# Two parts of a 48-row block in one stationary of 112 columns, and expert weights in longer runs

## The reference

```python
combine = ...                      # (1024, 16): top-1 of 4 groups, then the top-2 of its 4 experts, weights normalized
y = 0
for e in range(16):
    h = silu(t @ w_gate[e]) * (t @ w_up[e])       # 1024 x 1024 @ 1024 x 256, twice
    y = y + combine[:, e:e + 1] * (h @ w_down[e])  # 256 x 1024
x = layer_norm(ALPHA * x + y, g, b)
```

## Time and profile before

| | |
|---|---|
| runs | 981.41 us median of 3 (980.06 to 983.18) |
| profiled execution | 976.16 us, its span 974.4 us |
| PE busy | 940.6 us (97% of the span) |
| DVE busy | 590.8 us (61%) |
| ACT busy | 350.9 us (36%) |
| POOL busy | 193.4 us (20%) |
| chain that ended last | PE 42% of the span, DVE 3%, DMA 1% |
| mean granted clock | 0.990 |

### The profile page before, as it was taken

How to read it: one execution, slowest core, us unless ns; L and a number is a source line. 1 busy time by engine, 2 the same in 40 slices (tenths; PEclk the granted TensorE clock), 3 DMA queues, 4 the chain that set the end, 5 groups by cost and what they waited for, 6 DMA issues and landing times. The chain is left out here.

```text
span 974.4 us, 15658 instructions
## 1 busy us (share of the span) xinstructions
PE 940.6 (97%) x5655; PEld 797.9 (82%) x5655; DVE 590.8 (61%) x1263; ACT 350.9 (36%) x737; POOL 193.4 (20%) x256
## 2 busy tenths in 40 slices
PE   7999999999999999999999999999899999999994
PEld 6899888777768888888867888879789898989883
DVE  6744341588676776756665445568353567777675
ACT  6123031345574555400025333230322334444441
POOL 0013100112241120013210000005200233342344
PEclk9999999999998999999999999999999999999998
DMA  8122010001699501700223000045888988899972
GB/s 308 63 87 87 1 66 1 1 1 51 259 412 368 174 23 34 277 15 1 87 86 134 1 1 1 1 173 218 272 278 261 316 276 296 294 323 328 316 254 81
DMA packets 67278, 151.60 MB, mean 156 GB/s; under 512 B 8720, under 2 KB 16144, under 8 KB 67216
## 3 DMA queue, kind: packets, MB, share of 16 engines
q1 hardware_dynamic: 59920, 133.82, 39.4%
q0 software_dynamic: 7296, 16.95, 4.5%
HBM read 107.62 MB, written 52.03 MB: 164 GB/s over the span
## 5 line engine op out<-in xcount | busy, mean ns | idle before, releaser
L2001 PEld LDWEIGHTS h_ps<-xgT,e_gate_up 128*128 128x128 f32 x1024 | 155.6, 192 | 4.9 <-issue 2.6
L2001 PE MATMUL h_ps<-xgT,e_gate_up 128*128 128x176 f32 x1024 | 157.1, 315 | 2.5 <-DVEq L2109 2.5
L265 PE MATMUL unit_ps<-whi,xhi 128*128 128x512 f32 (+1 forms) x256 | 97.8, 382 | 6.1 <-DVE wlo L303 6.1
L267 PE MATMUL unit_ps<-whi,xlo 128*128 128x512 f32 (+1 forms) x256 | 97.5, 381 | 0.0
L266 PE MATMUL unit_ps<-wlo,xhi 128*128 128x512 f32 (+1 forms) x256 | 97.5, 381 | 0.0
L265 PEld LDWEIGHTS unit_ps<-whi,xhi 128*128 128x128 f32 x256 | 48.4, 189 | 14.1 <-DVE xlo L347 6.0
L2144 DVE SCALAR_TENSOR_TENSOR z<-y_ps,slot_weight,x_rows 128x512 f32<-128x512 f32 (+1 forms) x64 | 45.7, 746 | 22.2 <-PE y_ps L2015 22.1
L267 PEld LDWEIGHTS unit_ps<-whi,xlo 128*128 128x128 f32 x256 | 48.3, 189 | 7.7
L266 PEld LDWEIGHTS unit_ps<-wlo,xhi 128*128 128x128 f32 x256 | 48.4, 189 | 7.5
L2013 PE MATMUL y_ps<-e_dn_hi,h_hi 128*128 128x512 f32 (+1 forms) x128 | 51.9, 405 | 0.0
L2015 PE MATMUL y_ps<-e_dn_hi,h_lo 128*128 128x512 f32 (+1 forms) x128 | 50.2, 392 | 0.0
(11 more groups left out here) (346 smaller groups left out, 2133.3 us busy)
## 6 DMA issues: line engine op xcount, KB each, us to landing
e_gate_up<-w_gu SPq DMA_DIRECT2D x16, 2048.0 KB, 10.3
e_down_raw<-w_dn SPq DMA_DIRECT2D x16, 1024.0 KB, 6.2
slot_rows<-zeros SPq DMA_DIRECT2D x22, 522.0 KB, 6.2
slot_sums<-zeros SPq DMA_DIRECT2D x22, 512.0 KB, 6.3
x_rows<-slot_rows SPq DMA_DIRECT2D x16, 522.0 KB, 4.8
slot_sums<-z SPq DMA_DIRECT2D x16, 512.0 KB, 4.4
wraw<-w_in SPq DMA_DIRECT2D x24, 256.0 KB, 4.8
xraw<-xT SPq DMA_DIRECT2D x16, 256.0 KB, 5.0
```

Of the source, the lines that this page charges most:

```text
L265: pe.matmul(o, hi, whi[:, s, 0:w], start=(s == 0), stop=False)
L267: last = pe.matmul(o, lo, whi[:, s, 0:w], start=False, stop=(s == KD - 1))
L2001: end = pe.matmul(hps[:, m, gu * CAP:(gu + 1) * CAP], gate_up[:, b, s, w], xT[:, s, :], start=(s == 0), stop=(s == KD - 1))
```

## The change

In the down product, the two units of block 1 are computed otherwise. `h_hi` is now 240 columns wide for each f: 128 of block 0, 48 of block 1, 16 of zeros, and then 48 with the *low* part of block 1. One stationary of 112 columns (128 to 240) gives high x high in PSUM rows 0 to 47 and low x high in rows 64 to 111, in one matmul; high x low follows as a second one. So a unit of block 1 has 4 matmuls in place of 6. DVE makes z of such a unit in two steps, the second of which waits for the first, and makes `h_lo` in two pieces. The order of the units is kept, with block 1's low part under a semaphore of its own.

The expert weights are laid out in DRAM so that each partition reads runs of 4096 bytes; `paired` is the matching view of the same tiles in SBUF. SP waits for `placed_at` ahead of its stores, and fetches block c of the rows of n + 2 before it stores block c of z, no longer after both stores. Left out of the diff below: the names of two semaphores, the count of `stats_cleared` that ACT waits for (7 for 6), the slice `hhi[:, m, 0:CAP]` in ACT's copy, and the same `paired` in the function that is used only when an expert overflows its slots.

```diff
--- before.py
+++ after.py
@@ -1319,12 +1319,12 @@
             sp.dma_start(b[:], over(A["ln_xa_b"], [P, D])).then_inc(loaded, 16)
 
             sp.wait_ge(w_lo, XH)
-            sp.dma_start(k.e_dn[:], A["w_dn"][0].rearrange("s p n -> p s n")).then_inc(k.dn_loaded, 16)
+            sp.dma_start(paired(k.e_dn[:]), A["w_dn"][0].rearrange("s p n -> p s n")).then_inc(k.dn_loaded, 16)
             sp.dma_start(k.g3[:], over(A["ln_moe_g"], [P, D])).then_inc(k.gains_loaded, 16)
             sp.dma_start(k.b3[:], over(A["ln_moe_b"], [P, D])).then_inc(k.gains_loaded, 16)
             sp.wait_ge(q_sum, NT)
             for e in range(2):
-                sp.dma_start(k.e_gu[:, e], A["w_gu"][e].rearrange("s p n -> p s n")).then_inc(k.gu_loaded[e], 16)
+                sp.dma_start(paired(k.e_gu[:, e]), A["w_gu"][e].rearrange("s p n -> p s n")).then_inc(k.gu_loaded[e], 16)
 
         @block.tensor
         def _(pe):
...
@@ -1792,6 +1792,11 @@
 
 
 
+def paired(w):
+
+    return w.rearrange("p (s t) n -> p s (t n)", t=2)
+
+
 def experts(nc, k):
     at, A, cst = k.at, k.dram, k.cst
     B1 = CAP - P
...
@@ -1808,8 +1813,9 @@
     xT = k.xgT
     hh = at("h", 143, [P, 2, CAP])
     act_g = at("silu_g", 144.5, [P, 2, CAP])
-    hhi = at("h_hi", 146, [P, 2, CAP], f32r)
-    hlo = at("h_lo", 147.5, [P, 2, CAP], f32r)
+    LOW = P + 64
+    hhi = at("h_hi", 150, [P, 2, LOW + B1], f32r)
+    hlo = at("h_lo", 147.5, [P, 2, P], f32r)
     slot_id = at("slot_number", 149, [P, NE, 2])
     is_high = at("slot_is_high", 149.25, [P, 2, 2])
     where = at("slot_where", 149.28125, [P, 2, 2])
...
@@ -1872,8 +1879,8 @@
                 sp.wait_ge(sem, value)
                 sp.sem_inc(held_sp, 1)
 
-            def fetch(row, b):
-                for c in range(2):
+            def fetch(row, b, blocks=range(2)):
+                for c in blocks:
                     sp.dma_start(rows[b][0:ROWS[c], c, :], k.xs_dram[bass.ds(row + c * P, ROWS[c]), :]).then_inc(rows_loaded[b], 16)
 
             sp.wait_ge(k.rows_scattered, 16 * 2 * NT)
...
@@ -1885,17 +1892,17 @@
                 last = is_one_of_last(e, 1)
                 if not last:
                     hold(dn_lo_done, n(4, 4))
-                    sp.dma_start(dn_raw[:], A["w_dn"][bass.ds(n(1, 1), 1)].rearrange("a s p n -> p (a s) n")).then_inc(dn_loaded, 16)
+                    sp.dma_start(paired(dn_raw[:]), A["w_dn"][bass.ds(n(1, 1), 1)].rearrange("a s p n -> p (a s) n")).then_inc(dn_loaded, 16)
                 if not is_one_of_last(e, 2):
                     hold(gsum, n(2, 2))
-                    sp.dma_start(gate_up[:, b], A["w_gu"][bass.ds(n(1, 2), 1)].rearrange("a s p n -> p (a s) n")).then_inc(gu_loaded[b], 16)
+                    sp.dma_start(paired(gate_up[:, b]), A["w_gu"][bass.ds(n(1, 2), 1)].rearrange("a s p n -> p (a s) n")).then_inc(gu_loaded[b], 16)
                 hold(z_stored, n(32, 128))
+                hold(placed_at, n(1, 1))
                 for c in range(2):
                     hold(z_made, n(4, 2 * c + 6))
+                    if not is_one_of_last(e, 2):
+                        fetch(n(CAP, 2 * CAP), b, [c])
                     sp.dma_start(k.z_dram[bass.ds(n(CAP, c * P), ROWS[c]), :], z[c][:]).then_inc(z_stored, 16)
-                if not is_one_of_last(e, 2):
-                    hold(placed_at, n(1, 1))
-                    fetch(n(CAP, 2 * CAP), b)
 
             steps(sp, step)
 
...
@@ -2005,26 +2012,38 @@
                 else:
                     turn(1 - b, h(32, 32 * (1 + b)))
 
-                def down(u, f):
-                    c, j = UNITS[u]
+                def down(j, f):
                     w = 2 * f + j
-                    hi, lo = (t[:, f, c * P:c * P + ROWS[c]] for t in (hhi, hlo))
-                    out = yps[0:ROWS[c], BANK[u], :]
+                    hi, lo, out = hhi[:, f, 0:P], hlo[:, f, :], yps[:, BANK[j], :]
                     pe.matmul(out, hi, dn_hi[:, b, w, :], start=(f == 0), stop=False)
                     pe.matmul(out, hi, dn_lo[:, b, w, :], start=False, stop=False)
                     return pe.matmul(out, lo, dn_hi[:, b, w, :], start=False, stop=(f == 1))
 
+                def small_down(j, f):
+
+                    w, bank = 2 * f + j, BANK[2 + j]
+                    if f:
+                        pe.matmul(yps[0:B1, bank, :], hhi[:, f, P:CAP], dn_lo[:, b, w, :], start=False, stop=False)
+                    last = pe.matmul(yps[0:64 + B1, bank, :], hhi[:, f, P:LOW + B1], dn_hi[:, b, w, :], start=(f == 0), stop=(f == 1))
+                    if f == 0:
+                        last = pe.matmul(yps[0:B1, bank, :], hhi[:, f, P:CAP], dn_lo[:, b, w, :], start=False, stop=False)
+                    return last
+
                 pe.wait_ge(dn_lo_done, n(4, 4))
                 pe.wait_ge(hlo_done, n(2, 1))
-                for u, free in ((0, 4), (1, 2), (2, 3)):
-                    pe.wait_ge(z_made, n(4, free))
-                    down(u, 0)
+                pe.wait_ge(z_made, n(4, 4))
+                down(0, 0)
+                down(1, 0)
+                pe.wait_ge(small_lo_done, n(2, 1))
+                small_down(0, 0)
                 pe.wait_ge(hlo_done, n(2, 2))
-                for u in range(3):
-                    down(u, 1).then_inc(ysum, 1)
+                down(0, 1).then_inc(ysum, 1)
+                down(1, 1).then_inc(ysum, 1)
+                pe.wait_ge(small_lo_done, n(2, 2))
+                small_down(0, 1).then_inc(ysum, 1)
                 pe.wait_ge(z_made, n(4, 5))
-                down(3, 0)
-                down(3, 1).then_inc(ysum, 1)
+                small_down(1, 0)
+                small_down(1, 1).then_inc(ysum, 1)
 
             steps(pe, step)
 
...
@@ -2112,9 +2131,10 @@
             dve.memset(zsum[:], 0.0).then_inc(stats_cleared, 1)
             dve.memset(share[:], -1.0 / D).then_inc(stats_cleared, 1)
             dve.memset(rs[:], 1.0).then_inc(stats_cleared, 1)
+            dve.memset(hhi[:, :, CAP:LOW].bitcast(f32), 0.0).then_inc(stats_cleared, 1)
             for c in range(2):
                 dve.memset(tmp[c][:], 0.0).then_inc(stats_cleared, 1)
-            dve.wait_ge(stats_cleared, 6)
+            dve.wait_ge(stats_cleared, 7)
             split_down(0, lambda a, c: c)
             dve.wait_ge(k.gains_loaded, 32)
 
...
@@ -2124,7 +2144,9 @@
                     dve.wait_ge(silu, n(2, m + 1))
                     dve.tensor_tensor(hh[:, m, :], act_g[:, m, :], hps[:, m, CAP:2 * CAP], ALU.mult).then_inc(hmul, 1)
                     dve.wait_ge(hhi_done, n(2, m + 1))
-                    dve.tensor_tensor(hlo[:, m, :], hh[:, m, :], hhi[:, m, :].bitcast(f32), ALU.subtract).then_inc(hlo_done, 1)
+                    dve.tensor_tensor(hlo[:, m, :], hh[:, m, 0:P], hhi[:, m, 0:P].bitcast(f32), ALU.subtract).then_inc(hlo_done, 1)
+                    dve.tensor_tensor(hhi[:, m, LOW:LOW + B1], hh[:, m, P:CAP], hhi[:, m, P:CAP].bitcast(f32), ALU.subtract)\
+                       .then_inc(small_lo_done, 1)
                     if last:
                         put_out(g_, [m])
                 if not lowest(e) and not last:
...
@@ -2141,7 +2163,13 @@
                 for u, (c, j) in enumerate(UNITS):
                     r, f = slice(0, ROWS[c]), slice(512 * j, 512 * j + 512)
                     dve.wait_ge(ysum, n(4, u + 9))
-                    dve.scalar_tensor_tensor(z[c][:, f], yps[r, BANK[u], :], wgt[r, b, c:c + 1], rows[b][r, c, f], ALU.mult, ALU.add,
+                    rest = rows[b][r, c, f]
+                    if c:
+                        dve.scalar_tensor_tensor(z[c][:, f], yps[64:64 + B1, BANK[u], :], wgt[r, b, c:c + 1], rest, ALU.mult, ALU.add)\
+                           .then_inc(half_made, 1)
+                        dve.wait_ge(half_made, n(2, j + 1))
+                        rest = z[c][:, f]
+                    dve.scalar_tensor_tensor(z[c][:, f], yps[r, BANK[u], :], wgt[r, b, c:c + 1], rest, ALU.mult, ALU.add,
                                              accum_out=zsum[r, c, j:j + 1]).then_inc(z_made, 1)
                     if last and u == 1:
                         mean(0, n)
...
@@ -2416,9 +2444,10 @@
     a["memT"] = c(np.transpose(mem[0]))
     a["xa_wq"], a["xa_wk"], a["xa_wv"], a["xa_wo"] = c(xa_wq[0]), c(xa_wk[0]), c(xa_wv[0]), c(xa_wo[0])
     a["router_w"], a["router_bias"] = c(router_w), c(router_bias.reshape(1, NE))
-    a["w_gu"] = c(np.concatenate([expert_w_gate[0], expert_w_up[0]], axis=2)[RUN].reshape(NE, KD, P, 2 * DE))
-
-    a["w_dn"] = c(expert_w_down[0][RUN].reshape(NE, 2, P, 2, D // 2).transpose(0, 1, 3, 2, 4).reshape(NE, 4, P, D // 2))
+    a["w_gu"] = c(np.concatenate([expert_w_gate[0], expert_w_up[0]], axis=2)[RUN]
+                .reshape(NE, KD // 2, 2, P, 2 * DE).transpose(0, 1, 3, 2, 4).reshape(NE, KD // 2, P, 4 * DE))
+
+    a["w_dn"] = c(expert_w_down[0][RUN].reshape(NE, 2, P, D))
     a["ln_moe_g"], a["ln_moe_b"] = c(ln_moe_g), c(ln_moe_b)
     return a
 
```

(5 more changed lines are left out.)

4 lines of the change are left out of this document (2 added, 2 removed).

## The result

The changed kernel takes 991.43 us (median of 3 runs, 991.24 to 992.15), against 981.41: a ratio of 1.0107, 95% interval 1.0090 to 1.0123. It is slower, as forecast, by 10.0 us in place of 3.4, and lies above the range of 973 to 989. The profiled execution took 991.43 us, its span 989.6.

The account below looks back on a forecast made before the run. PE was taken to bound the kernel at 16.745 us an expert, a DVE-POOL loop having only 0.22 us of slack. Terms -4.36, +5.9, +0.3 and +1.6 gave +3.4 on 981.41: 984.8 us, range 973 to 989.

Parts of the forecast that it names:

- PE's saving and the early experts: PE's down product: 0.916 us less an expert, 0.09 stall added; early experts 15.92 us each, -4.36 us together.
- The z phase: On DVE, from the start of unit 0's z to the means: 4.31 us in place of 3.43, bounds 4.2 to 4.5.
- The loop: DVE and POOL waiting on each other: 17.40 us an expert, longer than PE's 15.92; +5.9 us over nine experts.
- Scatters slipping in: Rival on the DVE-POOL loop: scatters land early for some experts, 16.9 us an expert, no change overall; chance 0.13.
- rival 2: POOL's second gather lands late for the next z: 0.35 us more in each of 9 loops, +3.2, 988 us; chance 0.08.
- The last expert: Stretch between the z starts of experts 14 and 15: between 0 and +0.88 us, taken as +0.3.
- The end: Last z phase: two more dependent steps of 0.79 us each, ahead of the last mean: +1.6 us.
- The profile-to-median offset: Median of the runs before lay 5.25 us above the profiled execution's 976.16 us; carried over unchanged into the forecast.

Follow-up runs that it names:

- e13: The changed kernel with POOL made to wait for `dn_lo` before each copy of the slot weights from expert 4 on: 1002.58 us, 1.0233 of before.
- e14: e13 with an eighth of each gate/up load, so part of the products uses other weights: 991.97 us, 1.0123 of before.
- e10: The kernel before with two dependent z steps for block 1 (its weighted sum added twice), nothing else changed: 990.15 us, 1.0137 of before.
- e2: The kernel before with only the expert weights laid out in runs of 4096 bytes: 983.66 us, 1.0045 of before.
- e15: The kernel before with SP's new order of fetches and stores alone: 979.71 us, 1.0006 of before.
- e8: The changed kernel with DVE's centring (gain left out) and `dn_lo` (subtraction left out) given one SBUF input each: 971.70 us, 0.9924 of before.
- e9: The changed kernel with an eighth of each gate/up load, so part of the products uses other weights: 968.54 us, 0.9893 of before.
- e1: The changed kernel with the old weight layout and SP's old order, leaving the 112-column stationary and two z steps: 993.19 us, 1.0146 of before.

## Why the prediction was right in direction and wrong in size

- *PE's saving and the early experts* held: periods of 15.92 where 15.92 was given, and -4.0 for -4.36. The stationary of 112 columns is issued at the same spacing as the others.
- *The z phase* is 4.49 (844.60 to 849.10), at its upper bound of 4.5, not 4.31. The second step starts 0.78 after the first (846.07, 846.85), as taken. The rest is the way from an accumulating step to the first of a small unit: taken as 0.69 and 0.68, it is 0.79 and 0.78 (845.28 to 846.07, 846.85 to 847.63).
- *The loop* held in its sum, less so in its parts. Place ends at U + 17.63, 16.02, 17.59, 17.51, 17.58, 17.49, 17.59, 17.32, 17.42 in experts 5 to 13: 156.15 in all, 17.35 each, for 17.40. But only four are the copy held by `dn_lo` (5, 7, 9, 11). In two the ids are held instead (12, 13), in two rstd was there and `ln_out` waited for h at the lower clock (8, 10), and in one nothing came late but a held gather (6). So the sum is right partly by luck: expert 6 shows what a loop into which the copy slips costs, 16.02, and in 8 and 10 it was the low clock, in no step of the forecast, that brought it back to 17.5.
- *Scatters slipping in* was given as a relief. In five of the nine the copy gets in by U + 6.1, and in all five the ids or the first gather is then held to `dn_lo`'s end or 1 us past it. Only in expert 6 does it save much, some 1.6 us.
- **The step that failed** is rival 2, "the gather comes late", priced at 0.35 us a loop and given 0.08. It measured 7.84 us in 6 of 9 experts, on top of 156.15 + 0.3 (the step from place to z in three experts): 164.3. The working took landings of 4.6 to 5.0 and asked whether they still fitted into a slack of 0.03 to 0.43. It didn't ask when these gathers are issued against the load, and carried over landings that hold for a gather 1.0 us ahead of it. Before, the second gather is issued at U + 11.49, and SP's load at U + 12.50 (870.82). After, the saving on PE puts the load at U + 11.80 (837.82) and the longer loop puts that gather at U + 12.55. In five of the six experts the gather was so issued 0.2 to 0.8 us after the load, and from its issue to the start of the z that waited for it, it took 5.9 to 7.5 us; the sixth (expert 6, issued 0.8 ahead of the load) cost 0.3. That the load in flight makes the gathers late is shown by e13 and e14. That being issued after it is what counts is not shown: in e10 the load is where it was, four late gathers were issued 0.16 to 0.19 us ahead of it, and 6.5 to 6.8 us passed until their z; in e2 and e15 gathers issued 1.0 us or more ahead were late as well, by 2.18 and by up to 1.16. What a gather must meet to be late stays open.
- *The clock* was in no step. After three of PE's five longer stands for z the gate/up product took 0.77 to 1.68 us more.
- *The last expert*: +2.8 for +0.3. The scatters before it landed 3.7 us after POOL was done with them, 1.8 before, so the copy (961.01) met centring, the ids took 3.56 us, and `ln_out` waited 3.71 for rstd, where before only the second gather was held.
- *The end*: -1.0 for +1.6. Two dependent steps did add: from U to the end of POOL's last instruction it is 13.6 us after and 12.9 in e10, against 11.3. But the last scatter landed 2.5 us after that, 5.8 before. In e10, where it took 6.0, the whole is +1.7.
- *The profile-to-median offset* of 5.25, carried over, was no constant. U of expert 0 lies between 706.3 and 711.6 in these traces, with the same code ahead of it; before's profiled execution was a quick one and after's is its own median. The offset put 5.25 into the forecast and the later start 3.9 into the result, so together they took 1.4 us off the error: luck, and not a step that held.

The Trainium skill, SBUF — State Buffer, "Who interferes with whom", lets a VectorE instruction with one SBUF input pass beside a GpSimd instruction that reads SBUF, and not one with two: e8 agrees, 0.18 us against 3.19. The same section supposes, as inferred, that a `tensor_tensor` doesn't hold up descriptor generation. An indirect gather was held all the same: 3.08 us beside `dn_lo`, a `tensor_tensor` (861.38 in e9), against 0.94 in e8. It reads its ids from SBUF, and whether that read or the descriptors are held, no run here shows.

The Trainium skill, DMA: Bandwidth & Descriptors, "Queues, rings and completion order", was cited for late gathers behind larger packets. The lateness came, but with runs of 2048 bytes as well (e1, e10), so packet size isn't what these runs show as its cause; that longer runs add to it in the kernel before (e2) isn't excluded.

## What to carry to other kernels

Look for the second loop of nearly the same length as the bound, and before adding to it, ask not only whether a transfer's latency still fits, but what it will be in flight with once both ends have moved. A wait that guards a buffer should stand where the buffer is needed again, not where the work on it ends: here a late wait and a saving on PE gained nothing apart and 0.9% together. An order of transfers that measures as nothing must be measured again when the bound has moved.

## What the runs showed of the hardware that was not expected

- An indirect DMA on POOL, 0.93 to 1.14 us by itself, took up to 4.63 us (expert 6 of after) beside DVE steps with two SBUF inputs, and the conversion of ids 3.56 in place of 0.24.
- After PE had stood 2.43 us for z, its granted clock was 0.54 for 3.6 us; after a stand of 2.90 at the same place the product took its usual 9.71. What tells the two apart stays open.
- After a scatter of the same size POOL could go on 1.7 to 3.0 us later in e9, with an eighth of the load, and up to 6.5 in after (7.1 in before). The last one of the kernel landed 2.5, 5.8 or 6.0 us after POOL's last step; why it varies stays open.
